# A two-layer block on one Trainium2 core: output and down projections by seven block products instead of eight

## The reference

```python
merged = sigmoid(ga) * (attn @ w_attn_branch) + sigmoid(gc) * (conv @ w_conv_branch)   # 512 x 1024
h = x + merged @ w_out                        # output projection, 1024 x 1024
hn = rms_norm(h, ffn_norm)
gate, val = split(causal_conv(hn @ w_up, ffn_conv_w))     # 2 x 2816 columns
h = h + (silu(gate) * val) @ w_down           # down projection, 2816 x 1024
x = rms_norm(h, final_norm)                   # input of the second block
```

## Time and profile before

| | us |
|---|---|
| median of 3 runs | 1054.07 (1054.03 to 1054.26) |
| profiled execution, first to last instruction (span) | 1050.5 |
| around the span, to the median | 3.6 |
| PE busy | 1038.4 (99% of the span) |
| DVE busy | 593.9 (57%) |
| ACT busy | 445.9 (42%) |
| POOL busy | 51.0 (5%) |

### The profile page before, as it was taken

How to read it: one execution, slowest core, us unless ns; L and a number is a source line. 1 busy time by engine, 2 the same in 40 slices (tenths; PEclk the granted TensorE clock), 3 DMA queues, 4 the chain that set the end, 5 groups by cost and what they waited for, 6 DMA issues and landing times.

```text
span 1050.5 us, 13952 instructions
## 1 busy us (share of the span) xinstructions
PE 1038.4 (99%) x5453; PEld 846.1 (81%) x5453; DVE 593.9 (57%) x1110; ACT 445.9 (42%) x855; POOL 51.0 (5%) x71
## 2 busy tenths in 40 slices
PE   9999999999999999999999999999999999999997
PEld 7877778888888888888888888899888677777785
DVE  6466665445356666533466563553456673567757
ACT  5355542233345434431234442453244454556640
POOL 0000000000001100000000000125200001000000
PEclk9999999999999999999999999999999999999999
DMA  7421133222341842333122323334211222511012
GB/s 277 160 65 57 61 101 100 95 89 98 123 140 41 275 152 87 98 125 110 61 101 85 100 97 110 131 122 135 91 61 61 61 81 71 211 41 41 21 61 80
DMA packets 29106, 107.08 MB, mean 102 GB/s; under 512 B 3227, under 2 KB 3371, under 8 KB 28401
## 3 DMA queue, kind: packets, MB, share of 16 engines
q1 hardware_dynamic: 24864, 86.13, 24.8%
q0 software_dynamic: 4032, 19.96, 5.3%
q10 hardware_dynamic: 144, 0.10, 0.0%
HBM read 101.44 MB, written 7.36 MB: 104 GB/s over the span
## 4 chain that ended last, share of the span: by engine, by line
PE 88%; DVE 5%; ACT 4%; issue 2%; DMA 2%; DVEq 0%; SPq 0%; ACTq 0%
PE ps L780 26%; PE ps L782 25%; PE ps L781 25%; PE ps L1054 2%; PE ps L1222 2%; PE ps L1205 1%; PE ps L1187 1%; DMA raw<-wp 1%; ACT whi L1285 1%; PE ps L1143 1%; PE ps L1106 1%; ACT SC L1336 1%; PE ps L1175 1%; DVE wlo L1633 0%; DVE SC L1739 0%
## 5 line engine op out<-in xcount | busy, mean ns | idle before, releaser
L780 PE MATMUL ps<-XH,whi 128*128 128x512 f32 (+1 forms) x864 | 336.7, 390 | 0.6 <-DVE XL L1646 0.2
L782 PE MATMUL ps<-XH,wlo 128*128 128x512 f32 (+1 forms) x864 | 326.9, 378 | 0.0
L781 PE MATMUL ps<-XL,whi 128*128 128x512 f32 (+1 forms) x864 | 326.5, 378 | 0.0
L1633 DVE TENSOR_TENSOR wlo<-raw,whi 128x1024 fp32r<-128x1024 f32 (+1 forms) x158 | 191.6, 1218 | 166.7 <-ACT whi L1285 166.1
L1285 ACT CAST whi<-raw 128x1024 fp32r<-128x1024 f32 (+1 forms) x158 | 161.2, 1027 | 95.9 <-PE ps L782 70.5
L780 PEld LDWEIGHTS ps<-XH,whi 128*128 128x128 f32 x864 | 162.6, 188 | 43.0 <-issue 12.4
L782 PEld LDWEIGHTS ps<-XH,wlo 128*128 128x128 f32 x864 | 162.6, 188 | 31.2
L781 PEld LDWEIGHTS ps<-XL,whi 128*128 128x128 f32 x864 | 162.8, 188 | 27.8 <-issue 0.5
L780 PE MATMUL ps<-whi,GH 128*128 128x512 f32 x176 | 68.8, 391 | 0.0
L782 PE MATMUL ps<-whi,GL 128*128 128x512 f32 x176 | 68.5, 389 | 0.0
L781 PE MATMUL ps<-wlo,GH 128*128 128x512 f32 x176 | 68.5, 389 | 0.0
(11 more groups left out here) (305 smaller groups left out, 1333.1 us busy)
## 6 DMA issues: line engine op xcount, KB each, us to landing
raw<-wp SPq DMA_DIRECT2D x150, 512.0 KB, 3.5
vec_dram<-row_dram POOLq DMA_DIRECT2D x1, 3072.0 KB, 13.7
H<-x POOLq DMA_DIRECT2D x1, 2048.0 KB, 8.1
x_dram<-H POOLq DMA_DIRECT2D x1, 2048.0 KB, 8.8
A<-w1c POOLq DMA_DIRECT2D x2, 1024.0 KB, 6.3
A<-x_dram POOLq DMA_DIRECT2D x1, 2048.0 KB, 12.8
y<-A SPq DMA_DIRECT2D x8, 256.0 KB, 2.0
raw<-wp SPq DMA_DIRECT2D x4, 402.0 KB, 3.9
```

The costliest lines, as they stand in the source:

```text
L780: self.e.matmul(o, ah, bh, start=start, stop=False)
L781: self.e.matmul(o, ah, bl, start=False, stop=False)
L782: return self.e.matmul(o, al, bh, start=False, stop=stop)
L1633: self.e.tensor_tensor(wlo[BUF[i]][:, 0:w], raw[i % NR][:, 0:w], whi[BUF[i]][:, 0:w].bitcast(F), ALU.subtract).then_inc(sems["lo"], 1)
```

## The change

**Seven products.** A matrix product in 2 x 2 blocks takes eight block products; the changed kernel uses a scheme with seven, of sums of blocks (the form with seven products and fifteen additions). The activation is split into 2 x 256 tokens and 2 x 128 features for each pair of feature tiles, the weight into the same feature blocks and 2 x 512 columns. The output projection is one group (G = 0, 4 feature pairs), the down projection three (G = 1, 2, 3, with 4, 4 and 3 pairs): the feed-forward part now runs as 8 + 8 + 6 tiles. `wino(G, p, r)` is product p for row tile r of the half: 3 matmuls of 512 columns for each pair. Results are collected in PSUM: products 3, 5 and 6 go on in banks that DVE must first have added into H, or subtracted from it.

**Weight sums.** Products 1 and 4 use a block of the weight as it is, by SP's ring. The five other operands are formed in SBUF by transfers that POOL issues: a block is copied, further blocks are added by transfers with `accum_op=ALU.add` (tiles X and Y).

**Activation sums.** DVE makes four sums of 128 x 256 for each feature pair (`sums_of`), and ACT and DVE split the seven operands into MW or GW.

**Order.** The norm steps are laid between the products: the first two row tiles are complete after product 4, the last two after product 6.

The core of the diff (numbers of lines dropped):

```diff
+OPERAND = [0, 1, 4, 5, 6, 3, 2]
+WBANKS = [(6, 7), (4, 5), (3, 0), (6, 7), (3, 0), (6, 7), (6, 7)]
+INTO = [(0, 0), (0, 0), (1, 1), (0, 1), (0, 1), (1, 1), (1, 0)]
 def stages(en):
...
-    def rows_normed(m, rows):
-        for t in range(3):
-            rows(t)
-            if t == 2:
-                en.turn(m, 0)
-            en.norm_rest(m, t)
-        en.turn(m, 1)
-        rows(3)
-        en.norm_rest(m, 3)
-        en.turn(m, 2)
+    def product(G, p, between=None):
+        u = unit(G, p, 0)
+        en.split_all(u + 4)
+        en.wino(G, p, 0)
+        if between:
+            between(0)
+        en.split_all(u + 5)
+        en.wino(G, p, 1)
+        if between:
+            between(1)
+
+    def group(G, sums):
+        product(G, 0, sums)
+        en.wino_sums(G, 2)
+        product(G, 1)
+        product(G, 2)
+        en.wino_sums(G, 3)
+        product(G, 3)
+        en.wino_sums(G, 4)
+
+    def group_normed(G, m, sums):
+        group(G, sums)
+        product(G, 4)
+        en.eps_on(m, 0)
+        en.eps_on(m, 1)
+        en.norm_rest(m, 0)
+        en.norm_rest(m, 1)
+        product(G, 5)
+        en.eps_on(m, 2)
+        en.eps_on(m, 3)
+        u = unit(G, 6, 0)
+        en.split_all(u + 4)
+        en.wino(G, 6, 0)
+        en.turn(m, 0)
+        en.turn(m, 1)
+        en.split_all(u + 5)
+        en.wino(G, 6, 1)
+        en.norm_rest(m, 2)
+        en.norm_rest(m, 3)
 
     def first_three(m, i, tile, tiles):
         en.part(i, 0, 0)
+        en.turn(m, 2)
         en.part(i, 1, 0)
         en.turn(m, 3)
         en.part(i, 2, 0)
...
         class Tensor(Engine):
+            def wino(self, G, p, r):
+                t, n = WBANKS[p][r], OPERAND[p]
+                W = GW if G else MW
+                if p == 0:
...
+                else:
+                    self.wait_ge("res", added(G, {3: 0, 4: 2, 5: 3, 6: 5}[p], r))
+                at = 16 + 2 * FIRST_F[G] if G else 0
+                ts = slice(r * P, (r + 1) * P)
+                for s in range(2):
+                    i = unit(G, p, s)
+                    self.wait_ge("hi", i + 2)
+                    self.wait_ge("lo", i + 2)
+                    for m in range(2 * s, min(2 * s + 2, PAIRS[G])):
+                        self.wait_ge("gl", at + 4 * m + (1, 2, 3, 4, 4, 3, 2)[p])
+                        ws = slice((m % 2) * 512, (m % 2) * 512 + 512)
+                        f = self.mm3(ps[t][:, :], W[:, n, 0, m, ts], W[:, n, 1, m, ts], whi[BUF[i]][:, ws],
+                                     wlo[BUF[i]][:, ws], p < 3 and m == 0, m == PAIRS[G] - 1, True)
...
         class Scalar(Engine):
+            def wino(self, G, p, r):
+                if G in (0, LAST_G) and p in (1, 4, 5, 6):
+                    half, c = INTO[p]
+                    self.wait_ge("res", added(G, p, r))
...
+                    self.square(2 if G else 1, 2 * half + r, c, p in (4, 6), (UA if G else GA)[:, 0, 0, :])
...
         class Vector(Engine):
+            def wino(self, G, p, r):
...
+                if r:
+                    self.wait_ge("used", unit(G, p, 1) + 1)
+                else:
+                    self.wait_ge("tm", 3 + 7 * G + p + 1)
...
+                if p in (3, 5):
+                    self.e.tensor_tensor(h, h, ps[WBANKS[p][r]][:, :], ALU.subtract).then_inc(sems["res"], 1)
+                else:
+                    self.e.tensor_tensor(h, ps[WBANKS[p][r]][:, :], h, ALU.add).then_inc(sems["res"], 1)
...
+            def sums_of(self, X, parity, at):
+                (a11, a21), (a12, a22) = ((X[:, i, 0, 0:256], X[:, i, 0, 256:512]) for i in range(2))
+                s3, s1 = X[:, 0, 1, 0:256], X[:, 0, 1, 256:512]
+                s2, s4 = X[:, 1, 1, 0:256], X[:, 1, 1, 256:512]
+                self.wait_ge("gl", at)
+                if parity == 0:
+                    self.e.tensor_tensor(s3, a11, a21, ALU.subtract).then_inc(sems["ms"], 1)
+                else:
+                    self.e.tensor_tensor(s1, a21, a22, ALU.subtract).then_inc(sems["ms"], 1)
+                    self.wait_ge("ms", at + 2)
+                    self.e.tensor_tensor(s2, s1, a11, ALU.subtract).then_inc(sems["ms"], 1)
+                    self.wait_ge("ms", at + 3)
+                    self.e.tensor_tensor(s4, a12, s2, ALU.add).then_inc(sems["ms"], 1)
...
         class Gpsimd(Engine):
+            def wino_sums(self, G, k):
+                if k == 0:
...
+                elif k == 2:
+                    for s in range(2):
+                        self.wait_ge(f"wx{s}", 64 * G + 16)
+                        self.wait_ge("lo", unit(G, 0, s) + 2)
+                        self.add_x(G, B12, s, 2)
+                    for s in range(2):
+                        self.wait_ge(f"wx{s}", 64 * G + 32)
+                        self.add_x(G, B22, s, 3)
...
```

More of the change, by code:

```diff
@@ L121 @@
      ring((0, 1, 2, 6), [(SLOT_Q + i, 0, "rsc", i + 1) for i in range(5)]))
-ring((1, 2, 0), [(SLOT_FFN + hf * N_HALF + 2 * j + g, 0, "ub", 4 * (11 * hf + j) + 2 * g + 2)
-                 for hf in range(2) for j in range(11) for g in range(2)], {0: ("xl", 12)})
+for _G in (1, 2, 3):
+    ring((1, 2, 0), [(up_slot(f, g), 0, "ub", 4 * f + 2 * g + 2)
+                     for f in range(FIRST_F[_G], FIRST_F[_G] + TILES_OF[_G]) for g in range(2)],
+         {0: ("xl", 12)} if _G == 1 else {0: ("res", added(_G - 1, 4, 1))})
 ring((1, 0), [(at + i, 0, name, i + 1) for at, n, name in (
@@ L308, in stages @@
     for n in range(8):
+        if n == 5:
+            en.wino_sums(0, 0)
         for j in range(2):
@@ L311, in stages @@
             en.gate(n, j)
+            if j == 0 and n and n % 2 == 0:
+                for part in range(2):
+                    en.merge_sums(n // 2 - 1, part)
         slot(SLOT_GATE + 3 * n + 2)
@@ L315, in stages @@
         en.merge(n)
+    en.wino_sums(0, 1)
     en.begin_norm(1)
[L318 to L332 removed]
+    group_normed(0, 1, lambda part: en.merge_sums(3, part))
@@ L333, in stages @@
+    en.ffn()
+    for G in (1, 2, 3):
+        last = FIRST_F[G] + TILES_OF[G] - 1
+        for f in range(FIRST_F[G], last + 1):
+            if f == last - 2:
+                en.wino_sums(G, 0)
+                en.wino_sums(G, 1)
+            if f == 0:
+                first_three(1, SLOT_FFN, en.up, [(0, 0, 2), (0, 1, 2), (1, 0, 2)])
                 en.distances()
             else:
-                for g in range(1 if half == 0 and j == 1 else 0, 2):
-                    slot(SLOT_FFN + half * N_HALF + 2 * j + g)
-                    en.up(half, j, g, 0)
-                    en.up(half, j, g, 1)
@@ L339, in stages @@
-            en.glu(half, j)
-            if half == 0 and j == 10:
-                en.biases()
-        if half == 1:
-            en.begin_norm(2)
-        for c in range(2):
-            for g in range(6 if half == 0 or c == 0 else 3):
-                i = SLOT_FFN + half * N_HALF + 22 + 6 * c + g
-                slot(i)
-                if half == 1 and c == 1:
-                    en.split_all(i + (4, 5, 7)[g])
-                for t in range(4):
-                    en.down(half, c, g, t)
@@ L352, in stages @@
-    rows_normed(2, lambda t: en.down(1, 1, 5, t))
+                for g in range(1 if f == 1 else 0, 2):
+                    slot(up_slot(f, g))
+                    en.up(f, g, 0)
+                    en.up(f, g, 1)
+                    if g == 0 and f % 2 == 0 and f > FIRST_F[G]:
+                        for part in range(2):
+                            en.glu_sums(f // 2 - 1, part)
+            en.glu(f)
+            if f == 3:
+                en.biases()
+        if G < LAST_G:
+            group(G, partial(en.glu_sums, last // 2))
+            for p in range(4, 7):
+                product(G, p)
+        else:
+            en.begin_norm(2)
+            group_normed(G, 2, partial(en.glu_sums, last // 2))
```

495 lines of the change are left out of this document (315 added, 180 removed).

## The result

| | before | after |
|---|---|---|
| median, us (runs) | 1054.05 (1052.49 to 1054.26, 4) | 1078.11 (1074.81 to 1081.82, 4) |
| profiled span, us | 1050.5 | 1076.9 |
| ratio, 95% interval | | 1.0233 [1.0209, 1.0257] |

The change makes the kernel 24 us slower. The forecast was 1063 with a range to 1076: right in its sign, 15 us short in size.

A forecast was written before the change was run, and what follows sets the result against it. PE was taken to bound the kernel everywhere. New pauses of 29.9 us, less 20.4 of removed matmuls and 0.8 of old pauses, gave +8.7 on 1054.07, stated as 1063 us; range 1051 to 1076.

The forecast's parts named there:

- the term of the weight sums: All groups: adding transfers at 5 to 6.5 us fit, nothing counted; up to 3 us in group 0 left to range.
- the tight chain: X for product 3: refill, two adding transfers in a row, then ACT's cast; bears 7 to 7.6 us a transfer.
- late sums: Adding transfers of 9 us or more make X late for product 3 in every group; 1075 to 1091; chance 13%.
- The clock: TensorE falls to 1.2 GHz behind the longest two to four pauses, some 2 us each; 1067 to 1072; chance 10%.
- Up phases that cost nothing: Up phases: DVE's added 2.7 us per feature pair raises its load from 61% to some 73%; nothing counted.
- The starts: Start of each group: PE waits for product 1's first slot, 0.5, 1.1, 1.1 and 3.4 us, together 6.1.
- The pauses' sum: All new PE pauses: starts 6.1, product 3 3.05, tails 20.75; together 29.9 us.
- product 3 of group 0: Closed add, square, cast, subtraction chain beside product 1 makes product 3's slots late: 1.2 us, and 1.85 in group 3.
- product 6: Tails of groups 0 and 3: PE waits behind the first two row tiles' norm, 3.2 and 5.15 us.
- ahead of `part`: Tails of groups 0 and 3: PE waits for XL ahead of the first `part`, 3.25 and 4.55 us.
- ahead of the third `turn`: Tails of groups 0 and 3: PE waits for the third row tile's norm, 2.25 and 2.35 us.
- The faster rival: Tails of groups 0 and 3: add not behind the slot's cast and subtraction, tails under 12 us; 1049 us; chance 14%.

The follow-up runs named there:

- e2: Changed kernel with plain copies in place of the adding transfers, so the output is not the reference's; 1065.1 us, ratio 1.0107.
- e5: Changed kernel with each adding transfer adding only the left half of its columns, so the sums are incomplete; 1065.4 us, ratio 1.0103.
- e7: Changed kernel with product 0 reading ring loads and X's sums for product 3 added ahead of the group; 1065.0 us, ratio 1.0095.
- e1: Changed kernel with matmuls nobody reads put ahead of PE's six long waits to keep the clock up; 1077.0 us, ratio 1.0218.
- e3: Changed kernel with the norm's gain row loaded 130 us earlier; 1077.2 us, ratio 1.0210.
- e4: Changed kernel with last products' splits earlier and the first two row tiles' transposes ahead of product 6 in groups 0 and 3; 1082.8 us, ratio 1.0282.
- e10: e7 with ACT's cast ahead of its square, the gain row loaded early, and products 5 and 6 exchanged; 1059.8 us, ratio 1.0055.
- e11: e10 with product 1's slots in groups 1 to 3 cast ahead of the last up tile's end; 1058.2 us, ratio 1.0037.
- e14: e7 with cast ahead of square, early gain row, early product 1 slots, groups 1 to 3 reordered, norm behind product 5's first add; 1056.2 us.
- e15: e14 with ACT's cast put behind its square again, and nothing else; 1068.0 us, ratio 1.0131.
- e17: e14 with ACT's table load for group 3 moved from the group's start to behind the third product; 1056.4 us, ratio 1.0029.

## Why the prediction was wrong

**The step that failed** is the term of the weight sums: "That bears 7 to 7.6 us a transfer. So nothing is counted here", with group 0's six transfers "worth up to 3 us more, which I leave to the range". The duration taken, 5 to 6.5 us, is about the median of the rows after (6.1 and 6.3). But a median over all transfers is not that of the first in a queue. In group 0 two adds of X, two of Y and a gain row share the engines with the ring loads (the transfers fill 91% of the engines' time from 274.4 to 301.6 us), and the first two adds of X take 10.9 and 14.2 us. Cost: some 7 us in group 0 (62.5 less 55.4). The other half of it was not looked at: only X for product 3 was called the tight chain, while in groups 1 and 2 it is Y for product 5, a copy and an add behind product 2, that came late (ACT waited 4.9 us twice in group 1), and behind it X for product 6 (1.4 and 1.5 us). Cost: 2.6 and 3.2 us. Together 13 us of the 15 missed. e2 and e5 show that the adds' bytes cost this much; e7 shows for group 0 that an earlier start is as good. This is the rival "late sums", given 13%. It named product 3, and there its condition, 9 us a transfer, was met in group 0 only (4.0 to 8.5 us in groups 1 to 3); the add of X for product 6 took 12.3 to 14.7 us in groups 0, 1 and 2. That the measured 1078 lies within its 1075 to 1091 is therefore partly luck: it was priced by 3 to 7 us at product 3 in each of four groups.

**The clock** was a rival of its own with 10%, and the half pace came: 34 us of it. In the tails it was not the cause: with it mostly kept up the third `turn`s came no earlier, and the time fell by 1 us (e1). Behind the last norm it was, and the forecast has no term for it. From the fourth `turn` of the last group to the end every run has the same work, and takes 357.6 to 357.7 us in the eight profiles without half pace there (before, e3, e4, e10, e11, e14, e15, e17), 359.2 to 359.3 in the nine with 3.4 us of it, and 360.8 and 360.9 in the two with 6.8 (the changed kernel and e5). So the 3.1 us there are the clock's, and whether they come differs between kernels that are alike in this stage.

**What held.** 90 matmuls fewer, at the same pace where the clock is up. Up phases that cost nothing. The starts: 0.44, 0.91, 0.92 and 3.42 us, forecast 0.5, 1.1, 1.1, 3.4. The pauses' sum came out at 31.0 against 29.9, but that is luck, for the terms differ: product 3 of group 0 4.76 for 1.2 and that of group 3 none for 1.85; product 6 4.72 and 5.54 for 3.2 and 5.15; ahead of `part` none and 1.30 for 3.25 and 4.55; ahead of the third `turn` 1.81 twice for 2.25 and 2.35; and 4.7 us in groups 1 and 2 at products 5 and 6 that it did not have. The third `turn` of group 3 came 50.56 us after its start, forecast 50.6: two errors that cancel, pauses 5.2 us too long in the forecast (17.3 against 12.1) and a clock at 0.50 for 10.2 us, which it did not have. With plain copies the whole kernel takes 1065.1, 2 us over the forecast.

**The faster rival** rested on the chain not being closed. It was closed. Opened, with copies, it leaves 8.4 us of tail waits and 1054.7 us, where the rival had 1049 for under 12; 12.4 us of PE's work at half pace, 6.2 us lost, is what it did not reckon with.

**What stays open.** Why the clock falls behind the last norm. In the changed kernel it fell at 764.6, with PE busy, during 24 matmuls of two columns each, which before the change and in e14 ran at full clock (2.73 us, now 3.17). Why it falls in one and not in the other I did not try. Some 2 us of PE's busy time, beside the half pace, are not placed either. No version that computes everything beat the kernel before; the best, e14 and e17, are 0.3% over it.

## What to carry to other kernels

A matmul saved on a bound engine is worth its pace only if the operands for the shorter schedule cost less: here 20 us of PE were paid for with 40 transfers that take 1.8 times a copy's time, 24 more splits and a norm with less cover. A transfer's price is that of its queue at that moment, so follow each buffer from its last reader to its next, all of them, and look for an earlier start before a cheaper transfer. When an engine waits at half clock, first ask whether what it waits for would have come sooner.

## What was not expected of the hardware

An add issued by POOL takes 0.85 to 0.89 us of POOL, and 1.2 to 1.5 where it follows right behind another; a copy takes 0.53 to 0.59. On the transfer engines an add takes 1.8 times a copy's time, by the estimate above. In the changed kernel the clock fell in waits of 3.4 to 5.5 us, for 3.4 to 10.2 us, and stood at 1.00 behind both of 1.81 us. But in e2 and e14 it fell right behind the same wait of 1.8 us ahead of the third `turn` of group 0, and in e17 behind one of 1.93. One fall of the changed kernel had no wait ahead of it, here in two-microsecond windows (columns as in the earlier trace rows):

```profile
762.00:764.00 2.00, 2.00 (x19) 2.00 (x17) 0.00 (x0) 1.36 (x4) 1.92 (x2) 1.00 0.65 236
764.00:766.00 2.00, 2.00 (x12) 1.98 (x12) 0.32 (x2) 0.39 (x1) 1.61 (x6) 0.65 0.00 0
766.00:768.00 2.00, 2.00 (x6) 1.53 (x5) 1.00 (x1) 0.00 (x0) 1.48 (x3) 0.50 0.00 0
```

PE is busy in all three windows and has 19, then 12, then 6 matmuls in them.
